# A decoder step on one core: key pages scored in pairs of visits, their projection's turned tiles moved one page and one score visit later

## The chip, the cores and the metric

One core of one Trainium2 chip runs the whole program. The metric is the device time of one execution in microseconds (us), lower is better. Of the kernel before three executions were timed: 908.4, 908.85 and 910.18 us, median 908.85 us.

## What is computed

One inference step of a two-layer decoder over 256 prompt tokens and 8 sequences of 8 sample tokens, all in float32. Layer one is an mLSTM mixer with an MLP, layer two block-sparse attention with an MLP. The change touches the attention of the sample tokens over 64 cached pages of 128 tokens (8 sequences of 8 pages), and the key projection that runs in its gaps:

```
kv = x @ w_kv                              # new keys and values, 320 tokens
q = (x @ w_q_b[j]).reshape(B, L, H_B, HD_B)
k_past = cache_k[page_table]               # 64 pages, 128 tokens x 8 heads x 128
page_sums = k_past.astype(F32).sum(2)      # block means choose 3 of 4 past blocks
lg_sel = einsum('bqhd,bqhrkd->bqhrk', q, sel_k) * scale - slope * dist
p = softmax(concatenate([lg_sel, lg_own])) # then times the value pages
```

## The kernel before

Activations lie transposed (features on partitions, T = 320 tokens along the free dimension). Each float32 product of a dense layer is three products of rounded parts: `dense` (L614 on) makes an output tile of 128 features from 8 chunks, each with a matmul high x high (L624), low x high (L625) and high x low (L626), 24 in all. ScalarE rounds a weight tile (`w_hi`, L1232), VectorE subtracts to get the rest (`w_lo`, L1636). Each of the five engines has its own hand-written queue, executed in order; semaphores tie the queues together.

The stretch of the change is the **key-page stage**. Pages come by DMA, issued by SyncE in a fixed order, into a ring of places. For page P TensorE does eight 128x128 transposes (`turn_page`, L1019), four heads into each of two PSUM banks; ScalarE copies the first bank into `k_turned` (`k_copy`, L1523), VectorE the second (L2031). Two pages are a *pair* (p = P // 2). `k_turned` has two buffers, one for even and one for odd pairs, so the copy of a page of pair p waits until pair p-2 is scored (`s_sc`). `score_pair` (L1061) multiplies the turned keys of one pair with the padded queries: matmuls whose weights are 32 columns wide, four heads side by side in the array, into banks 4 to 7. In the profile a score visit is 16 matmuls, in four groups of four.

In the gaps, for n = 0 to 7, `k_extra` makes head n of the new keys: at pair 2 + 2n TensorE runs the dense tile n of the key weights (*key tile*). VectorE then runs three operations on its bank (`kvq`, L1988 to L1990; only the first two read the bank), ScalarE adds the bias (`kvq` on its own queue, L1476), and one pair later (pair 3 + 2n) TensorE transposes the result in three pieces (`turn3`, L638 to L640: the *turned key tile*), which ScalarE copies out and stores with two DMAs that it issues itself (`kv_out`, L1461 to L1466). At pair 18 `own_scores` (L1030) stands in place of a key tile. Also on VectorE's queue here: logits of the first group of scores after pages 33 and 35 (L2058, L2060), a block maximum after page 39 (L2067, L2068), a dozen small operations after page 41 (L2074 to L2090), and after the even pages 10 to 24 a part of the residual is rebuilt (L1873 to L1877).

All transposes, key tiles, turned key tiles and own scores take their banks from one rotation over banks 0 to 3, the *slots*, in the order of the list `SLOTS`. Slot i may be written when what stood in slot i-4 has been read:

```
def slot_free(p, k):
    i = SLOT[p, k]
    if i >= 4:
        pe.wait_ge(*slot_read(*SLOTS[i - 4]))
```

`slot_read` says which semaphore tells of that reading: ScalarE's or VectorE's copy of a page half, for a key tile `s_uk` (raised after VectorE's third operation), for a turned key tile `s_tc`.

The order on TensorE before, for a pair p: both pages of p are turned, pair p-1 is scored, and then comes a key tile (even p from 2 to 16) or a turned key tile (odd p from 3 to 17).

After this stage come the value pages: `page_values` (L1119) uses each value page, the value projection runs in its gaps, then the rest of the layer.

Of the kernel before, what the change touches and what calls it, by code (L numbers as in the profile page):

```python
# [22 lines left out]
T = TP + TS  # L23
# [50 lines left out]


K_FIRST = 2
SLOTS = [(p, k) for p in range(NPG // 2) for k in range(5) if k < 4 or K_FIRST <= p <= K_FIRST + 16]
SLOT = {pk: i for i, pk in enumerate(SLOTS)}


# [82 lines left out]
def build(nc, x_prompt, x_sample, state_C, state_n, state_m, cache_k, cache_v, page_table,  # L163
# [4 lines left out]
    with ctx:  # L168
# [159 lines left out]
        def sem(name):  # L328
            return ctx.enter_context(nc.semaphore(name))
# [52 lines left out]
            sem(n) for n in ("k_copied_act", "k_copied_dve", "probs_turned_n", "probs_copied", "x_hi_prompt",  # L382
                             "o_scaled", "o_turned", "attn_out")]
        s_nm = sem("new_m")
        s_out = sem("stored")
        s_co, s_po = sem("c_stored"), sem("prompt_state_stored")

# [33 lines left out]
        def slot_read(p, k):  # L421

            if k < 4:
                return (s_kA, s_kD)[k % 2], 2 * p + k // 2 + 1
            n = (p - K_FIRST) // 2
            if n == 8:
                return s_ownr, 1
            return (s_uk, 8 + n + 1) if (p - K_FIRST) % 2 == 0 else (s_tc, n + 1)

        def emptied(t):  # L430

# [177 lines left out]
        def _(pe):  # L609
# [400 lines left out]
            def turn_page(P):  # L1010

                pe.wait_ge(s_in[PAGE_AT[P]], 16 * PAGE_LOADS[P])
                for half in range(2):
                    k = 2 * (P % 2) + half
                    slot_free(P // 2, k)
                    bank = slot_bank(P // 2, k)
                    for j in range(4):
                        h = 4 * half + j
                        last = nc.tensor.transpose(bank[:, 128 * j:128 * j + 128],  # L1019
                                                   page[PAGE_AT[P]][:, 128 * h:128 * h + 128], ident)  # L1020
                    last.then_inc((s_half, s_used)[half], 1)
# [13 lines left out]
            def k_extra(p):  # L1035

                n, odd = divmod(p - K_FIRST, 2)
                if p == K_FIRST + 16:
                    own_scores(p)
                elif odd:  # L1040
                    slot_free(p, 4)
                    pe.wait_ge(s_ev[0], evac(8 * Q_WK + n)[1])
                    turn3(slot_bank(p, 4), KA[:, n, :]).then_inc(s_tp, 1)
                else:
                    i = SLOT[p, 4]
                    dense(8 * Q_WK + n, XH, XL, None, TW, slot_read(*SLOTS[i - 4]))

            def score_pair(pair):

                G, bb, r = pair // 16, pair // 4 % 4, pair % 4  # L1050
                pe.wait_ge(s_kA, 2 * pair + 2)
                pe.wait_ge(s_kD, 2 * pair + 2)
                if pair % 16 == 0:
                    pe.wait_ge(s_qz, G + 1)
                if pair == 0:
                    pe.wait_ge(s_uk, 8)
                if pair in (16, 18):
                    pe.wait_ge(s_Lr, 2 + pair - 16)
                for a_ in range(2):
                    for j in range(4):  # L1060
                        last = mm(ps[SCORE_BANK[2 * a_ + r // 2]][32 * j:32 * j + 32,  # L1061
                                                                  256 * (r % 2):256 * (r % 2) + 256],
                                  QZ[G][:, 4 * a_ + j, bb, :], KT[pair % 2][:, 4 * a_ + j, :],
                                  start=(bb == 0 and r % 2 == 0), stop=True, skip_group_check=True)
                last.then_inc(s_sc, 1)
# [76 lines left out]

            for pair in range(NPG // 2):
                turn_page(2 * pair)
                turn_page(2 * pair + 1)
                if pair >= 1:
                    score_pair(pair - 1)
                if K_FIRST <= pair <= K_FIRST + 16:
                    k_extra(pair)
            score_pair(NPG // 2 - 1)  # L1150
            probs_turn(0)
            v_tile(0)
# [60 lines left out]
        def _(act):  # L1213
# [360 lines left out]
            for P in range(NPG):  # L1574
                p = P // 2
                k_copy(P)
                if P == 0:
                    kvq(7)
                if P in (1, 3):
                    q_lay(P // 2)  # L1580
                if P % 2 and K_FIRST <= p <= K_FIRST + 16:
                    k_extra(p)
                if 45 <= P < 55:
                    exp_step(0, P - 45)
# [42 lines left out]
        def _(dve):  # L1627
# [353 lines left out]
            def kvq(i):  # L1981

                t = 8 * Q_WQ + i
                u, bank = UK[i % 2], dense_bank(t)
                dve.wait_ge(s_mm, t + 1)
                if i >= 2:
                    dve.wait_ge(s_ev[0], evac(t - 2)[1])
                V.tensor_scalar(cb[:, t % 4:t % 4 + 1], bank[:, T + 1:TW], QSCALE if i < 8 else 1.0, None, ALU.mult)  # L1988
                own(V.scalar_tensor_tensor(u[:, :], nmu[:, :], bank[:, T:T + 1], bank[:, 0:T], ALU.mult, ALU.add))
                V.tensor_tensor(u[:, :], u[:, :], rs[:, :], ALU.mult).then_inc(s_uk, 1)  # L1990

            for i in range(8):
# [322 lines left out]
```

## Time and profile before

| | |
|---|---|
| timed executions | 908.4, 908.85, 910.18 us (median 908.85) |
| profiled execution, its own span | 909.7 us |
| key-page stage, first transpose to last score | 423.09 to 548.89 us of the span |
| TensorE matmuls busy | 896.8 us (99%) |
| TensorE weight loads busy | 838.1 us (92%) |
| VectorE / ScalarE busy | 622.7 us (68%) / 438.1 us (48%) |
| bytes moved | 182.78 MB, mean 201 GB/s |

The profile is of one execution. Times in its views count from the start of the span. In a row of the timeline, `x16` merges 16 instructions of one form, the first number is the start of the first, the second the time from there to the end of the last; what stands in brackets is idle time of the engine before it and what ended it. Matmuls overlap, so the distance between two starts tells what one costs, not its length. PE is TensorE, PEld its weight loads, DVE VectorE, ACT ScalarE, SP SyncE; a q behind a name is the engine's queue of instructions that issue or wait.

### The profile page before, as it was taken

The numbers are of one execution on the slowest core, as the hardware profiler recorded it, in microseconds if no ns is written. First come the engines' busy times: TensorE is split into PE (matmuls) and PEld (weight loads), VectorE is DVE, ScalarE is ACT, GpSimd is POOL, SyncE is SP. The second block draws the span as 40 slices with busy tenths as digits, with TensorE's granted clock in tenths as the row PEclk, the third lists the DMA queues.
The fourth block names the chain that finished last, engine by engine and source line by source line (L and its number), as shares of the span: only waits on it lengthen the run. The fifth ranks groups of instructions, "written<-read, shape, count | busy, mean of one in ns | idle before, by whom it ended". The sixth has DMA issues, their size and how long they took to land.

```text
span 909.7 us, 18709 instructions
## 1 busy us (share of the span) xinstructions
PE 896.8 (99%) x7472; PEld 838.1 (92%) x7472; DVE 622.7 (68%) x1089; ACT 438.1 (48%) x826; POOL 64.7 (7%) x81
## 2 busy tenths in 40 slices
PE   9999999999999999999999999999999999999996
PEld 8999988999999999999888878987999999999985
DVE  6477568788976575677575847446578897757536
ACT  5445666476345363445344453345447644526421
POOL 0010006500000000330000000000230000000000
PEclk9999999999999999999999999999999999999999
DMA  9982215664454444566988997998944545454401
GB/s 285 265 250 95 94 48 138 188 196 140 140 178 146 139 142 159 167 219 231 334 292 282 360 373 283 399 400 352 284 144 144 179 132 195 148 169 148 139 1 59
DMA packets 132331, 182.78 MB, mean 201 GB/s; under 512 B 5875, under 2 KB 113211, under 8 KB 132244
## 3 DMA queue, kind: packets, MB, share of 16 engines
q1 hardware_dynamic: 126938, 177.56, 59.0%
q0 software_dynamic: 640, 2.10, 0.9%
q10 hardware_dynamic: 4666, 1.92, 0.8%
q8 instruction: 60, 0.98, 0.4%
q14 instruction: 27, 0.22, 0.1%
HBM read 175.24 MB, written 6.32 MB: 200 GB/s over the span
## 4 chain that ended last, share of the span: by engine, by line
PE 94%; DMA 2%; SPq 1%; ACT 1%; DVE 1%; issue 1%; DVEq 0%
PE ps L624 24%; PE ps L626 23%; PE ps L625 23%; PE ps L1019 7%; PE ps L1061 4%; PE ps L1119 2%; DMA page<-in_cache_v_dram 2%; PE ps L907 1%; PE ps L909 1%; PE ps L908 1%; SPq L535 1%; SPq L542 1%; DMA x_tok<-in_x_prompt_dram 1%; PE ps L638 1%; PE ps L741 0%
## 5 line engine op out<-in xcount | busy, mean ns | idle before, releaser
L1232 ACT ACTIVATE w_hi<-raw 128x1024 fp32r<-128x1024 f32 x192 | 202.4, 1057 | 227.2 <-PE ps L626 204.4
L1636 DVE TENSOR_TENSOR w_lo<-raw,w_hi 128x1024 fp32r<-128x1024 f32 x192 | 237.4, 1240 | 102.7 <-ACT w_hi L1232 102.6
L624 PE MATMUL ps<-x_hi,w_hi 128*128 128x322 f32 (+1 forms) x888 | 279.8, 315 | 0.0
L626 PE MATMUL ps<-x_hi,w_lo 128*128 128x322 f32 (+1 forms) x888 | 276.5, 311 | 0.0
L625 PE MATMUL ps<-x_lo,w_hi 128*128 128x322 f32 (+1 forms) x888 | 276.1, 311 | 0.0
L624 PEld LDWEIGHTS ps<-x_hi,w_hi 128*128 128x128 f32 x888 | 168.1, 189 | 5.2 <-ACT k_turned L1523 2.9
L624 PE MATMUL ps<-h_hi,w_hi 128*128 128x320 f32 x552 | 170.9, 310 | 0.0
L626 PE MATMUL ps<-h_hi,w_lo 128*128 128x320 f32 x552 | 170.5, 309 | 0.0
L625 PE MATMUL ps<-h_lo,w_hi 128*128 128x320 f32 x552 | 170.4, 309 | 0.0
L625 PEld LDWEIGHTS ps<-x_lo,w_hi 128*128 128x128 f32 x888 | 168.8, 190 | 0.2
L626 PEld LDWEIGHTS ps<-x_hi,w_lo 128*128 128x128 f32 x888 | 167.6, 189 | 0.0
L624 PEld LDWEIGHTS ps<-h_hi,w_hi 128*128 128x128 f32 x552 | 103.8, 188 | 3.4 <-DVE x L1804 1.7
L625 PEld LDWEIGHTS ps<-h_lo,w_hi 128*128 128x128 f32 x552 | 103.8, 188 | 0.0
L626 PEld LDWEIGHTS ps<-h_hi,w_lo 128*128 128x128 f32 x552 | 103.7, 188 | 0.0
L1019 PE MATMUL ps<-base,page 128*128 128x128 f32 x512 | 63.1, 275 | 0.0
L1019 PEld LDWEIGHTS ps<-base,page 128*128 128x128 f32 x512 | 56.3, 141 | 7.1 <-issue 5.3
L2031 DVE COPY k_turned<-ps 128x512 f32<-128x512 f32 x64 | 43.8, 690 | 24.7 <-PE ps L1019 23.6
L1523 ACT ACTIVATE k_turned<-ps 128x512 f32<-128x512 f32 x64 | 36.1, 591 | 29.9 <-PE ps L1019 29.9
L1969 DVE TENSOR_TENSOR x<-x,ps 128x320 f32<-128x320 f32 x56 | 27.2, 487 | 31.8 <-PE ps L626 30.8
L1413 ACT ACTIVATE fm<-fm 128x320 f32<-128x320 f32 x64 | 29.4, 459 | 19.2 <-DVE fm L1936 19.1
L1934 DVE SCALAR_TENSOR_TENSOR fm<-ln_neg_mu,ps 128x320 f32<-128x320 f32 x64 | 35.0, 546 | 3.8 <-PE ps L626 3.7
L1936 DVE SCALAR_TENSOR_TENSOR fm<-ln_std,ps,fm 128x320 f32<-128x320 f32 x64 | 35.6, 556 | 2.3
(347 smaller groups left out, 978.7 us busy)
## 6 DMA issues: line engine op xcount, KB each, us to landing
raw<-in_w_up_dram SPq DMA_DIRECT2D x32, 1024.0 KB, 5.8
raw<-in_w_down_dram SPq DMA_DIRECT2D x32, 1024.0 KB, 5.2
page<-in_cache_k_dram SPq DMA_DIRECT2D x64, 512.0 KB, 5.7
page<-in_cache_v_dram SPq DMA_DIRECT2D x64, 512.0 KB, 9.4
raw<-in_w_in_a_dram SPq DMA_DIRECT2D x11, 1024.0 KB, 8.7
raw<-in_w_kv_dram SPq DMA_DIRECT2D x8, 1024.0 KB, 6.6
raw<-in_w_out_a_dram SPq DMA_DIRECT2D x4, 1024.0 KB, 5.2
raw<-in_w_q_b_dram SPq DMA_DIRECT2D x4, 1024.0 KB, 5.4
```

Source lines behind the costliest of these rows:

```text
L624: mm(out, WH[PLACE[t]][:, k, :], hi[:, k, 0:width], start=(k == 0), stop=False)
L625: mm(out, WH[PLACE[t]][:, k, :], lo[:, k, 0:width], start=False, stop=False)
L626: last = mm(out, WL[PLACE[t]][:, k, :], hi[:, k, 0:width], start=False, stop=(k == 7))
L1019: last = nc.tensor.transpose(bank[:, 128 * j:128 * j + 128], page[PAGE_AT[P]][:, 128 * h:128 * h + 128], ident)
L1061: last = mm(ps[SCORE_BANK[2 * a_ + r // 2]][32 * j:32 * j + 32, 256 * (r % 2):256 * (r % 2) + 256], QZ[G][:, 4 * a_ + j, bb, :], KT[pair % ...
L1232: A(WH[PLACE[t]][:, :, :], raw_tile(t), ACT.Copy)\
L1413: own(A(f[:, :], f[:, :], ACT.Relu))
L1523: A(KT[P // 2 % 2][:, 0:4, 128 * (P % 2):128 * (P % 2) + 128], slot_bank(P // 2, 2 * (P % 2))[:, :].rearrange("p (h t) -> p h t", h=4), AC ...
L1636: V.tensor_tensor(WL[PLACE[t]][:, :, :], raw_tile(t), WH[PLACE[t]][:, :, :].bitcast(F32), ALU.subtract)\
L1934: own(V.scalar_tensor_tensor(f[:, :], nmu[:, :], bank[:, T:T + 1], bank[:, 0:T], ALU.mult, ALU.add))
L1936: V.scalar_tensor_tensor(f[:, :], sd[:, :], bank[:, T + 1:TW], f[:, :], ALU.mult, ALU.add)\
L2031: V.tensor_copy(KT[P // 2 % 2][:, 4:8, 128 * (P % 2):128 * (P % 2) + 128], slot_bank(P // 2, 2 * (P % 2) + 1)[:, :].rearrange("p (h t) -> ...
```

## The change

TensorE visits the scores once in two pairs. At an even pair p (from 2 on) the order becomes: first page of p turned; pair p-2 and pair p-1 scored; the turned key tile that stood behind pair p-1; second page of p turned; the key tile. At an odd pair only its two pages are turned. The last visit scores pairs 30 and 31, as before. `SLOTS` and the queues of ScalarE and VectorE follow that order. A new semaphore `s_kb` is raised by VectorE's second operation on a key tile (the last that reads the bank) and takes the place of `s_uk` in `slot_read`.

```
 K_FIRST = 2
-SLOTS = [(p, k) for p in range(NPG // 2) for k in range(5) if k < 4 or K_FIRST <= p <= K_FIRST + 16]
+SLOTS = []
+for _p in range(NPG // 2):
+    SLOTS += [(_p, 0), (_p, 1)]
+    if K_FIRST < _p <= K_FIRST + 16 and _p % 2 == K_FIRST % 2:
+        SLOTS.append((_p - 1, 4))
+    SLOTS += [(_p, 2), (_p, 3)]
+    if K_FIRST <= _p <= K_FIRST + 16 and _p % 2 == K_FIRST % 2:
+        SLOTS.append((_p, 4))
...
-            return (s_uk, 8 + n + 1) if (p - K_FIRST) % 2 == 0 else (s_tc, n + 1)
+            return (s_kb, n + 1) if (p - K_FIRST) % 2 == 0 else (s_tc, n + 1)
...
             for pair in range(NPG // 2):
                 turn_page(2 * pair)
+                if pair % 2 == 0 and pair:
+                    score_pair(pair - 2)
+                    score_pair(pair - 1)
+                if pair % 2 == 0 and K_FIRST < pair <= K_FIRST + 16:
+                    k_extra(pair - 1)
                 turn_page(2 * pair + 1)
-                if pair >= 1:
-                    score_pair(pair - 1)
-                if K_FIRST <= pair <= K_FIRST + 16:
+                if pair % 2 == 0 and K_FIRST <= pair <= K_FIRST + 16:
                     k_extra(pair)
+            score_pair(NPG // 2 - 2)
             score_pair(NPG // 2 - 1)
...
-                if P % 2 and K_FIRST <= p <= K_FIRST + 16:
+                if P % 2 == 0 and p % 2 == 0 and K_FIRST < p <= K_FIRST + 16:
+                    k_extra(p - 1)
+                if P % 2 and p % 2 == 0 and K_FIRST <= p <= K_FIRST + 16:
                     k_extra(p)
...
-                own(V.scalar_tensor_tensor(u[:, :], nmu[:, :], bank[:, T:T + 1], bank[:, 0:T], ALU.mult, ALU.add))
+                ins = V.scalar_tensor_tensor(u[:, :], nmu[:, :], bank[:, T:T + 1], bank[:, 0:T], ALU.mult, ALU.add)
+                if 8 <= i < 16:
+                    ins.then_inc(s_kb, 1)
+                    dve.wait_ge(s_kb, i - 7)
+                else:
+                    own(ins)
```

**TensorE, behind a key tile.** Twelve rows before, from the first transpose after a key tile: `page2` and `page3` are the two pages of one pair, `k_turned`, `w_hi` and so on the tiles of the section above, ps0 to ps3 the four rotating banks.

```order
L1019 MATMUL ps3<-base_78,page2_134 128x128 [waits k_copied_dve,page_in2]
L1019 MATMUL ps3<-base_78,page2_134 128x128 x3
L1019 MATMUL ps0<-base_78,page2_134 128x128 [waits k_copied_act]
L1019 MATMUL ps0<-base_78,page2_134 128x128 x3
L1019 MATMUL ps1<-base_78,page3_135 128x128 [waits k_copied_dve,page_in3]
L1019 MATMUL ps1<-base_78,page3_135 128x128 x3
L1019 MATMUL ps2<-base_78,page3_135 128x128 [waits kvq_scaled]
L1019 MATMUL ps2<-base_78,page3_135 128x128 x3
L1061 MATMUL ps4<-k_turned0_128,q_padded0_170 32x256 [waits k_copied_dve,k_copied_act]
L1061 MATMUL ps4<-k_turned0_128,q_padded0_170 32x256 x3
L1061 MATMUL ps5<-k_turned0_128,q_padded0_170 32x256 x4
L638 MATMUL ps3<-base_78,k_attn_68 128x128 [waits act_emptied,k_copied_act]
```

The same place in the changed kernel (its lines are 8 higher):

```order
L1027 MATMUL ps3<-base_78,page2_134 128x128 [waits turn_copied,page_in2]
L1027 MATMUL ps3<-base_78,page2_134 128x128 x3
L1027 MATMUL ps0<-base_78,page2_134 128x128 [waits k_copied_act]
L1027 MATMUL ps0<-base_78,page2_134 128x128 x3
L1027 MATMUL ps1<-base_78,page3_135 128x128 [waits k_copied_dve,page_in3]
L1027 MATMUL ps1<-base_78,page3_135 128x128 x3
L1027 MATMUL ps2<-base_78,page3_135 128x128 [waits k_bank_read]
L1027 MATMUL ps2<-base_78,page3_135 128x128 x3
L1027 MATMUL ps3<-base_78,page4_136 128x128 [waits k_copied_act,page_in4]
L1027 MATMUL ps3<-base_78,page4_136 128x128 x3
L1027 MATMUL ps0<-base_78,page4_136 128x128 [waits k_copied_dve]
L1027 MATMUL ps0<-base_78,page4_136 128x128 x3
```

The score visit that stood behind `page3` is gone from there, and `page4` follows at once (two score visits stand behind it), into ps3, the bank that `page2`'s first half took eight transposes before.

**ScalarE, the same stretch** (of the first cycle, whose banks have other numbers). Before: bias of the key tile, the two copies of the next pair, the copy-out of the turned key tile and its DMAs, the next copy.

```order
L1476 ACTIVATE k_attn_68<-kvq0_179,b_times_w_81 128x320 [waits kvq_scaled]
L1523 ACTIVATE k_turned1_129<-ps1 128x4x128 [waits pair_scored,page_half_turned]
L1523 ACTIVATE k_turned1_129<-ps3 128x4x128 [waits pair_scored,page_half_turned]
L1461 ACTIVATE turned0_158<-ps1 128x256 [waits turn_done]
L1462 ACTIVATE turned0_158<-ps1 64x128
L1464 DMA out_5_dram<-turned0_158 128x2x128 [waits turn_copied]
L1466 DMA out_10_dram<-turned0_158 64x128
L1523 ACTIVATE k_turned0_128<-ps2 128x4x128 [waits pair_scored,page_half_turned]
```

In the changed kernel (lines 12 higher):

```order
L1488 ACTIVATE k_attn_68<-kvq0_179,b_times_w_81 128x320 [waits kvq_scaled]
L1535 ACTIVATE k_turned1_129<-ps1 128x4x128 [waits pair_scored,page_half_turned]
L1535 ACTIVATE k_turned1_129<-ps3 128x4x128 [waits pair_scored,page_half_turned]
L1535 ACTIVATE k_turned0_128<-ps1 128x4x128 [waits pair_scored,page_half_turned]
L1473 ACTIVATE turned0_158<-ps3 128x256 [waits turn_done]
L1474 ACTIVATE turned0_158<-ps3 64x128
L1476 DMA out_5_dram<-turned0_158 128x2x128 [waits turn_copied]
L1478 DMA out_10_dram<-turned0_158 64x128
```

The copy-out of the turned key tile stands one page copy later, and ps1 is read twice by page copies with one copy between them.

## Rows read from the trace of the kernel before

**Rows 1.** Windows (stretch, length, busy time of each engine, clock, DMA share, GB/s).

```profile
503.61:548.89 45.28, 45.28 (x534) 33.58 (x531) 28.47 (x52) 22.74 (x53) 0.00 (x0) 1.00 0.97 371
552.00:556.00 4.00, 4.00 (x58) 3.81 (x60) 3.97 (x8) 1.90 (x4) 0.00 (x0) 1.00 0.16 65
560.00:620.00 60.00, 58.82 (x1001) 52.58 (x1004) 30.14 (x89) 22.82 (x64) 2.31 (x8) 1.00 1.03 395
```

**Rows 2.** Timeline of TensorE over one cycle of two pairs, pages 10 to 13.

```profile
444.26 2.05 PE L1019 MATMUL ps<-base,page 128*128 128x128 f32 x16
446.25 1.07 PE L1061 MATMUL ps<-k_turned,q_padded 128*32 128x256 f32 x16
447.25 0.33 PE L638 MATMUL ps<-base,k_attn 128*128 128x128 f32 x1
447.41 0.27 PE L639 MATMUL ps<-base,k_attn 128*128 128x128 f32 x1
...
447.63 1.92 PE L1019 MATMUL ps<-base,page 128*128 128x128 f32 x16
449.48 1.07 PE L1061 MATMUL ps<-k_turned,q_padded 128*32 128x256 f32 x16
450.48 0.41 PE L624 MATMUL ps<-x_hi,w_hi 128*128 128x322 f32 x1
450.74 0.31 PE L625 MATMUL ps<-x_lo,w_hi 128*128 128x322 f32 x1
450.88 0.31 PE L626 MATMUL ps<-x_hi,w_lo 128*128 128x322 f32 x1
```

**Rows 3.** Timeline: second and last group of four of one score visit.

```profile
446.48 0.40 PE L1061 MATMUL ps<-k_turned,q_padded 128*32 128x256 f32 x4
446.92 0.40 PE L1061 MATMUL ps<-k_turned,q_padded 128*32 128x256 f32 x4
```

**Rows 4.** Waits, 423 to 549 us (who <- for whom: us in total, times, longest).

```profile
PEld ps L1019 <- DVE kvq L1990: 1.3, 8, 0.2
```

**Rows 5.** Timeline of VectorE and ScalarE behind the key tile that ends at 444.26.

```profile
444.46 0.16 DVE L1988 TENSOR_SCALAR b_times_w<-ps 128x1 f32<-128x1 f32 x1 [1.61 <-PE ps L626]
444.54 0.54 DVE L1989 SCALAR_TENSOR_TENSOR kvq<-ln_neg_mu,ps 128x320 f32<-128x320 f32 x1
445.11 0.49 DVE L1990 TENSOR_TENSOR kvq<-kvq,ln_rstd 128x320 f32<-128x320 f32 x1
...
445.64 0.56 ACT L1476 ACTIVATE k_attn<-kvq,b_times_w 128x320 f32<-128x320 f32 x1 [4.05 <-DVE kvq L1990]
446.11 1.06 ACT L1523 ACTIVATE k_turned<-ps 128x512 f32<-128x512 f32 x2
```

**Rows 6.** Timeline of ScalarE: copies after the turned key tile, next weight tile.

```profile
449.43 1.09 ACT L1523 ACTIVATE k_turned<-ps 128x512 f32<-128x512 f32 x2 [1.06 <-PE ps L1019]
450.40 1.06 ACT L1232 ACTIVATE w_hi<-raw 128x1024 fp32r<-128x1024 f32 x1
```

**Rows 7.** Timeline of VectorE around the last key tile: first logits, weight tile, key tile.

```profile
500.09 0.69 DVE L2058 TENSOR_REDUCE soft_small<-ps 128x2 f32<-128x512 f32 x1 [0.34 <-PE ps L1061]
...
502.61 1.22 DVE L1636 TENSOR_TENSOR w_lo<-raw,w_hi 128x1024 fp32r<-128x1024 f32 x1
503.81 0.16 DVE L1988 TENSOR_SCALAR b_times_w<-ps 128x1 f32<-128x1 f32 x1
```

**Rows 8.** Timeline of VectorE: copies of pages 40 to 43 and what stands between them.

```profile
512.89 2.28 DVE L2067 TENSOR_REDUCE soft_small<-logits 128x8 f32<-128x2048 f32 x1
...
515.39 1.29 DVE L2031 COPY k_turned<-ps 128x512 f32<-128x512 f32 x2
...
518.53 1.28 DVE L2031 COPY k_turned<-ps 128x512 f32<-128x512 f32 x2
```

**Rows 9.** Timeline of TensorE: the own scores.

```profile
509.71 0.63 PE L1030 MATMUL ps<-k_attn,q_attn 128*32 128x64 f32 x32
```

**Rows 10.** Waits of SyncE's queue, 552 to 640 us.

```profile
SPq L542 <- PE ps L1119: 5.7, 1, 5.7
```

More of the change, by code:

```diff
@@ L384, in build @@
         s_nm = sem("new_m")
+        s_kb = sem("k_bank_read")
         s_out = sem("stored")
```

## Prediction

> **What bounds the kernel now.** I read the windows first, then TensorE's timeline, then the queues that feed it. Over the last part of the key-page stage TensorE is busy in every microsecond, at the full 2.4 GHz (granted clock 1.00) [rows 1]: the stage lasts as long as TensorE's own queue, so I price the change there. Its timeline [rows 2] shows one cycle of two pairs: 16 transposes from 444.26, a score visit from 446.25, the turned key tile from 447.25, 16 transposes from 447.63, a visit from 449.48, and the next key tile from 450.48. The reader is to look at distances between starts. In the steady stream a transpose costs 0.11 us. Where a full-width stream changes to the 32-column scores and back, the distances grow, though the views call the engine busy: 16 transposes take 447.63 to 449.48, 1.85 us, where 16 x 0.109 would be 1.74.
>
> One real wait stands in this stretch: 1.3 us in eight waits of TensorE for VectorE's third operation on a key tile [rows 4]. It is the last quarter of the first block, 444.26 to 446.25 = 1.99 us against 1.85 for the other block.
>
> **What a merged visit saves.** Entering the scores costs 1.85 - 1.74 = 0.10. Inside a visit the groups are (446.92 - 446.48) / 2 = 0.22 apart, but from the last group to the next full-width matmul it is 447.25 - 446.92 = 0.33: 0.11 for leaving [rows 2, 3]. The first transpose after it takes 0.16 instead of 0.11 (447.25 to 447.41), 0.05; the first matmul of a key tile 0.26 instead of 0.15 (450.48, 450.74, 450.88), 0.11 [rows 2]. The visit's first group is longer by 0.02. So one change of width and back costs 0.29 before transposes, 0.33 before a key tile. Before there are 31 such excursions; after it 16 visits and one for the own scores, which then stand between transposes. 14 fewer; eight of them preceded a key tile: 14 x 0.29 + 8 x 0.04 = **-4.4 us**.
>
> What this draining is, the Trainium skill says ("TensorEngine Tiling (Array Packing)", Key Properties): changing the tiling mode drains the array. "TensorE: Matmul & The Clock Gate" (Single matmul latency) gives the part of a lone matmul that is not streaming as (398/2.4) = 166 ns; at that price for each of 28 changes of mode the gain would be an estimated 4.6 us, about what the rows give.
>
> **What the early signal saves.** VectorE's second operation ends at 444.54 + 0.54 = 445.08, the third at 445.11 + 0.49 = 445.60 [rows 5]. TensorE wants that bank after 12 transposes, at 444.26 + 1.30 = 445.56; it is free at 445.08 plus a signal of 0.05. The whole wait goes: the blocks' difference 1.99 - 1.85, up to 0.16 with rounding, eight times: **-1.2 us**. Behind the waiting instruction VectorE has nothing new, since it waited for its own second operation before too.
>
> **What the new order makes wait.** Here I follow the banks. Behind a key tile three pages are now turned in a row: the second and third slot of the rotation are fine, but the first bank of the third page (page 2p+4, for a key tile at pair p) is the one that the first half of page 2p+2 took eight transposes earlier, and it may be written only when ScalarE has copied that half. ScalarE's copy stands behind its bias of the key tile, and that one waits for VectorE's *third* operation, which the new semaphore does not make earlier. From the end of the key tile (444.26): third operation ends +1.34, bias starts +1.38, the two copies start at +1.85 [rows 5]. Two copies take 1.06 with 0.60 for one of them alone, so the first ends at about +2.44, and its signal reaches TensorE at +2.49. TensorE wants the bank after 16 transposes, at +1.74. It waits 0.75, and the first transpose after a wait pays the 0.05 of a restart: 0.80. Before, a score visit (1.00) and a different bank lay between, which is why this copy never showed as a wait. There are eight key tiles. Seven of these waits are alike: 7 x 0.80 = **+5.6 us**.
>
> **The eighth key tile** is worse. VectorE's queue has four logits operations and a weight tile between the copy of page 33 and this key tile: 500.09 to 502.61 and on to 503.81, 3.72 us, and before they ended just as the key tile did [rows 7]. They could start while page 33's score visit still ran. Now the key tile starts right after page 33's transposes. VectorE's copy of that page starts 0.20 later (the lag by which 444.46 follows 444.26) and frees the engine after 0.60 [rows 8]; then 3.72: it reaches the key tile's bank at +4.52 after the tile's start, where a tile of 24 matmuls, 0.15 apart, would have it at 3.60 + 0.20 = 3.80. Everything behind is 0.72 late. The second bank of page 35 is then wanted at +1.30 and free at 0.82 + 0.05 + 0.72 = 1.59, a wait of 0.29 and a restart; the first bank of page 36 is wanted at 1.74 + 0.34 = 2.08 and free at 2.49 + 0.72 = 3.21: 1.13 and a restart. Together **+1.5 us**.
>
> **Two single waits after it.** ScalarE issues the last turned tile's stores itself; in the present order it is free for a copy 449.43 - 447.25 = 2.18 after that tile starts [rows 2, 6]. Now page 37, the own scores and page 38 follow directly: the second bank of page 38 is wanted at 0.38 + 0.87 + 0.10 + 0.50 + 0.11 + 0.49 = 2.45 (the own scores take 0.63 to the end of the last, some 0.50 without its tail [rows 9]) and page 37's copy out of it ends at 2.18 + 0.60 + 0.05 = 2.83: about **+0.4**. And VectorE's block maximum and its dozen small operations after pages 39 and 41: from the start of the maximum to the next copy 518.53 - 512.89 = 5.64 [rows 8], with the copy of page 39 before it (0.20 + 0.60) and that of page 42 after (0.69 + 0.05) 7.18 less overlaps, about 7.0. TensorE had 7.3 of work there with three visits; now it has page 40, one double visit (2.0), pages 41 to 43 and a half, 5.9 up to the second bank of page 44, which page 42 must have left: about 1.1 to 1.35, I take **+1.3**.
>
> In the rest of the stage four pages in a row take 3.5 us, and VectorE's copies are 0.60 apart (1.29 for two, 0.69 for one) under the 0.87 of a page: no wait. ScalarE's exponentials fit with them.
>
> **The sum.** -4.4 - 1.2 + 5.6 + 1.5 + 0.4 + 1.3 = +3.2; walking all three queues through the whole stage by the same durations gives +3.5. I take +3.4.
>
> **Does it reach the end?** Behind the stage the DMA engines fall idle (share 0.16) and then run full (1.03) for 60 us [rows 1]: the value pages' loads set the end of that stage. They begin when the first value page has been used: SyncE's queue waits 5.7 us there [rows 10]. That use moves with the key-page stage, so the loads start as much later, and the delay reaches the end whole.
>
> The profiled execution took 909.7, 0.85 above the median of 908.85; +3.4 gives 913.1 by the profile, **912.3 us** by the median. A measurement of this kernel tells 0.2%, 1.8 us, from no change.
>
> **Rivals.**
> *The wait on ScalarE's copy does not come (faster).* If the copy of page 2p+2 ended by +1.7, the 7 x 0.80 and some 0.8 of the eighth tile's would go: 3.2 - 6.4, -3.2, 905.7 us. The sign turns below a wait of about 0.35 per cycle. For it: the start of the copies is read behind a queue order that I take as unchanged. Against: the rows of the order show bias, then copy, on ScalarE, and the bias waits for the same semaphore as before. 0.07.
> *The two sides cancel.* The seven waits come, but the late VectorE terms (1.5 - 0.8, 0.4, 1.3) don't, and the visits save a little more, 0.33 each: -4.6 - 1.2 + 6.4, +0.6, 909.4 us. For it: they rest on margins of some tenths. Also that the value stage takes the delay up: were its loads not started by the stage's end, nothing would be seen. Together 0.17.
> *The key tile's own turn comes late each cycle (slower still).* ScalarE now rounds the next weight tile after the stores of the turned tile and one more copy: from my walk at 8.05 after the key tile's end, 1.06 long, then VectorE's 1.22 to 10.36, and the next key tile's result is wanted at 10.2 + 0.2 [rows 5 to 7]. The margin is 0.03 us; where the stores take 0.3 more, each cycle is 0.3 longer: 6 x 0.3, +5.2, 914.1 us. For it: nothing pulls the queue back. Against: 450.40 follows 449.43 by 0.97 throughout, so the durations hardly vary. 0.14.
>
> **How the numbers follow.** The forecast (slower by about 3.4) has 0.62, the slower rival 0.14: slower 0.76. Cancelling has 0.17, faster 0.07. The range leaves out the fast rival and part of the cancelling one: 909.2 (half the forecast sum undone and a low draw) to 914.8 (the slow rival and a high draw of the runs).
>
> **What would show it.** Right: eight new waits of TensorE before a transpose, ended by ScalarE's page copy, 0.7 to 0.8 each; the eight waits for VectorE's third operation gone; excursions to the scores 16; cycles of 10.2 us instead of 9.9; one wait of over 1 us for VectorE near page 44; the value stage moved as a whole. Wrong: cycles of 9.4 us (no bank wait), or a key stage longer by 3 us and an end that is not.

## The result and the profile after

The changed kernel took 913.03 us (median of seven executions, 912.19 to 916.63) against 909.71 us (seven, 908.4 to 911.18) for the kernel before in the same series: ratio 1.0042, interval 1.0028 to 1.0056. It is slower by 3.3 us; 912.3 and +3.4 were forecast. The profiled execution is one of its two longest, 916.63 us, with a span of 914.8, so every term below is read from stretches and not from the whole. (A span is 1.8 or 1.9 shorter than its execution's time in every run here. The span of 909.7 that the prediction started from thus belongs to a time near 911.5, and its "0.85 above the median" compared a span with a time.)

The stage from the first page's transpose to the first use of a value page grew from 555.05 - 423.09 = 131.96 to 560.29 - 422.94 = 137.35 us: +5.4 in this execution. TensorE's timeline of the cycle that answers to [rows 2], pages 10 to 13:

```profile
444.04 0.31 PE L634 MATMUL ps<-x_hi,w_lo 128*128 128x322 f32 x1
444.19 1.91 PE L1027 MATMUL ps<-base,page 128*128 128x128 f32 x16
446.83 1.06 PE L1027 MATMUL ps<-base,page 128*128 128x128 f32 x8 [0.73 <-ACT k_turned L1535]
447.82 1.93 PE L1069 MATMUL ps<-k_turned,q_padded 128*32 128x256 f32 x32
449.69 0.33 PE L646 MATMUL ps<-base,k_attn 128*128 128x128 f32 x1
...
450.07 1.04 PE L1027 MATMUL ps<-base,page 128*128 128x128 f32 x8
450.86 0.39 PE L632 MATMUL ps<-x_hi,w_hi 128*128 128x322 f32 x1
...
454.50 0.27 PE L1027 MATMUL ps<-base,page 128*128 128x128 f32 x1
```

The double visit runs from 447.82 to 449.69, 1.87 us; two single ones took 2.00 and their entries besides. That is the gain. The loss is the bracket, idle time ahead of the row's first transpose: 16 transposes behind the key tile TensorE stands for ScalarE's copy. From key tile's end to key tile's end it is 454.50 - 444.19 = 10.31 us, 9.88 before (444.26 to 454.14). ScalarE's side:

```profile
445.64 0.56 ACT L1488 ACTIVATE k_attn<-kvq,b_times_w 128x320 f32<-128x320 f32 x1 [2.35 <-DVE kvq L2009]
446.11 1.07 ACT L1535 ACTIVATE k_turned<-ps 128x512 f32<-128x512 f32 x2
```

These are the rows of before [rows 5] almost to the hundredth: ScalarE has not moved, TensorE has come to want its copy earlier. The waits of the stage (423 to 560 us; us in total, times, longest):

```profile
PEld ps L1027 <- issue: 10.7, 15, 1.2
...
PE ps L1027 <- ACT k_turned L1535: 6.4, 9, 1.0
...
PEld ps L1069 <- issue: 3.0, 17, 0.3
...
PEld ps L1027 <- DVE kvq L2003: 1.5, 2, 0.8
...
PE ps L1027 <- DVE k_turned L2050: 1.1, 1, 1.1
PE ps L1027 <- DVE kvq L2003: 1.0, 2, 0.6
```

TensorE's timeline has 16 score visits in the stage; the third row counts their entries and one stop of 0.33 within the last visit. The wait for VectorE's third operation [rows 4] is gone; the second operation (L2003) ends two. Nine waits for ScalarE's copies have come. The single ones stand where the prediction put them, behind the eighth key tile (508.94 and 510.64), in page 38 and in page 44:

```profile
508.94 0.66 PE L1027 MATMUL ps<-base,page 128*128 128x128 f32 x4 [0.59 <-DVE kvq L2003]
510.64 1.06 PE L1027 MATMUL ps<-base,page 128*128 128x128 f32 x8 [1.04 <-ACT k_turned L1535]
...
516.31 2.40 PE L1027 MATMUL ps<-base,page 128*128 128x128 f32 x20 [0.23 <-ACT k_turned L1535]
...
524.93 0.66 PE L1027 MATMUL ps<-base,page 128*128 128x128 f32 x4 [1.14 <-DVE k_turned L2050]
```

One cycle is longer than its sisters, 464.75 - 454.50 = 10.25 being followed by 11.3. ScalarE's and VectorE's rows there:

```profile
461.50 1.68 ACTq L1478 DMA_DIRECT2D out_dram<-turned  x1
463.28 0.60 ACT L1535 ACTIVATE k_turned<-ps 128x512 f32<-128x512 f32 x1 [2.23 <-issue]
463.78 1.05 ACT L1244 ACTIVATE w_hi<-raw 128x1024 fp32r<-128x1024 f32 x1
```

```profile
464.86 1.23 DVE L1650 TENSOR_TENSOR w_lo<-raw,w_hi 128x1024 fp32r<-128x1024 f32 x1 [2.73 <-ACT w_hi L1244]
466.00 0.15 DVE L2002 TENSOR_SCALAR b_times_w<-ps 128x1 f32<-128x1 f32 x1
```

The issue of the second store held ScalarE for 1.68 us, where it mostly takes 0.50. The copy, the weight tile and its rest follow one after another, and VectorE reaches the finished key tile (464.75) at 466.00, 1.05 late. TensorE's 24 transposes there take 4.61 instead of 3.56. A second such issue, 1.83 at 503.62, makes the eighth key tile's share larger by 0.5 (4.75 here, 4.24 in e4 and e5 below). Together these two make 1.5 us of this execution's loss.

Behind the stage nothing is given back in this pair of profiles: the value pages take 642.65 - 560.29 = 82.36 us from first to last, 637.52 - 555.05 = 82.47 before, with the DMA engines full [rows 1] (mean share 1.03 in this window too), and SyncE's queue waits as long as in [rows 10]:

```profile
565.00:625.00 60.00, 58.81 (x999) 52.67 (x997) 30.38 (x89) 22.60 (x63) 2.32 (x8) 1.00 1.03 391
```

```profile
SPq L550 <- PE ps L1127: 5.7, 1, 5.7
```

In the profiles of the experiments below this distance lies between 81.0 and 82.6 us, with no relation to the length of the stage before it. So a part of the delay of up to about one microsecond could be given back without being seen here.

### The profile page after: what moved, and what is told of

Read it like the earlier page. It is cut to its first block, busy times and chain, and to the rows that moved or that the text cites. A ratio compares the mean times of both kernels' runs of the same rounds, so it can differ in the third digit from the quotient of the medians.

```text
span 914.8 us, 18709 instructions
## 1 busy us (share of the span) xinstructions
PE 894.4 (98%) x7472; PEld 839.7 (92%) x7472; DVE 622.1 (68%) x1089; ACT 438.8 (48%) x826; POOL 64.8 (7%) x81
## 4 chain that ended last, share of the span: by engine, by line
PE 90%; ACT 2%; DVE 2%; issue 2%; DMA 2%; SPq 1%; ACTq 1%; DVEq 0%; POOL 0%; POOLq 0%
PE ps L632 23%; PE ps L634 23%; PE ps L633 23%; PE ps L1027 4%; PE ps L1069 3%; PE ps L1127 2%; DMA page<-in_cache_v_dram 2%; ACT k_turned L1535 1%; PE ps L915 1%; PE ps L917 1%; PE ps L916 1%; ACTq L1478 1%; PE ps L646 1%; PE ps L663 1%; PE ps L749 0%
```

## The experiments

All eleven were timed; each median stands beside that of the kernel before in the same series. Line numbers in the fences are each kernel's own. "Stage" is the distance from the first page's transpose to the first value page's use in the profiled execution: 131.96 before, 137.35 with the change.

**The change in two halves.** First the early signal alone, in the old order.

```
# kernel before, with the new semaphore only
-            return (s_uk, 8 + n + 1) if ...
+            return (s_kb, n + 1) if ...
...
+                if 8 <= i < 16:
+                    ins.then_inc(s_kb, 1)
...
```

> The kernel before with the early signal alone (VectorE's second operation frees the key tile's bank), order unchanged. My theory: the eight waits of TensorE before the second bank of the page behind a key tile go, 0.10 to 0.16 us each: 0.9 to 1.2 us faster than before. Rival (the wait is only moved to the next slot, or the value stage's loads set the end anyway): no difference, the key-page stage as long as before.

Measured: 908.41 us against 909.9, ratio 0.999 (0.9977 to 1.0003); stage 131.39, 0.57 shorter, about half of what was expected. All eight waits are gone (16 transposes behind a key tile 1.84 instead of 1.99), but in four cycles the *other* block grew from 1.84 to 2.00. TensorE and VectorE in one of them:

```profile
445.11 2.06 PE L1020 MATMUL ps<-base,page 128*128 128x128 f32 x16
```

```profile
444.26 0.55 DVE L1875 SCALAR_TENSOR_TENSOR x<-x,ln_cols_alpha,ln_rstd 128x320 f32<-128x320 f32 x1
444.85 0.39 DVE L1878 TENSOR_SCALAR x<-x,ln_cols_alpha 128x320 f32<-128x320 f32 x1
445.27 0.69 DVE L2037 COPY k_turned<-ps 128x512 f32<-128x512 f32 x1
```

The rebuilt piece of the residual stands between two copies. TensorE's own wait had hidden it; with the wait gone the copy at 445.27 is the late one. Then the new order alone, with the old signal:

```
# changed kernel, without s_kb
-            return (s_kb, n + 1) if ...
+            return (s_uk, 8 + n + 1) if ...
...
-                if 8 <= i < 16: ...
+                own(V.scalar_tensor_tensor(u[:, :], ...))
```

> The changed kernel without the early signal: the new order alone. My theory: the second bank of page 2p+3 is late again by 0.15, but the wait for ScalarE's copy before page 2p+4 ends at the same moment as with the signal and swallows it: as slow as the changed kernel (3 to 3.5 us over before), waits for ScalarE's copy 0.6 instead of 0.75 each. Rival (the signal has its full worth in the new order): 1.2 us slower than the changed kernel, 4.5 over before.

Measured: 912.91 us, ratio 1.004 (1.0025 to 1.0054), no different from the whole change. The 24 transposes behind a key tile take the same 3.56 in six of the eight cycles (4.28 behind a store issue that was held 1.36, and 4.25 behind the eighth key tile). TensorE's idle time before ScalarE's copy is 0.51 instead of 0.66: the two delays end at the same copy. The late signal costs nothing here: whatever TensorE loses on it in the second page, it would have lost a little later waiting for ScalarE. In the new order the signal's 1.2 us are not a gain at all, and the order alone is what makes the kernel slower.

**The disputed wait removed.** ScalarE's bias of the key tile moves behind the copy of the first half of the page that follows next.

```
# changed kernel; ScalarE's queue
-                    kvq(8 + n)
...
             k_copy(P)
+            if P % 2 == 0 and p % 2 and K_FIRST < p <= K_FIRST + 15:
+                kvq(8 + (p - 1 - K_FIRST) // 2)
```

> The changed kernel with one move on ScalarE's queue: the copy of page 2p+2 stands ahead of the key tile's bias. My theory (the loss is ScalarE's copy standing behind a bias that waits for VectorE's third operation): the eight waits for ScalarE go, 5.6 to 6.4 us; four cycles in which VectorE rebuilds a residual chunk between two copies then make the second score visit wait 0.5 each, +2.1: in sum 4 to 4.5 faster than the changed kernel, about 1 us faster than before. Rival (the loss is the merged visit itself, or the DMA queues): no change against the changed kernel, 3 to 3.5 over before, the waits reappear under another name.

Measured: 908.97 us against 909.9, ratio 0.9993 (0.998 to 1.0006), about 4 us below the change. The wait for ScalarE's copy is gone in all eight cycles: 24 transposes take 2.71, not 3.56, in six of them. The fourth (3.50, behind a store issue held 1.55) and the eighth (3.27) still wait for VectorE's late turn at the key tile. And in four cycles a new wait stands within the double visit, here 445.63 - 444.12 = 1.51 for the first half in place of 0.89:

```profile
444.12 1.07 PE L1069 MATMUL ps<-k_turned,q_padded 128*32 128x256 f32 x16
445.63 1.07 PE L1069 MATMUL ps<-k_turned,q_padded 128*32 128x256 f32 x16 [0.44 <-DVE k_turned L2051]
```

```profile
443.27 0.48 DVE L1888 TENSOR_TENSOR x<-x,ln_neg_mu 128x320 f32<-128x320 f32 x1
...
444.80 1.29 DVE L2051 COPY k_turned<-ps 128x512 f32<-128x512 f32 x2
```

It is the rebuilt piece again (443.27 to 444.80), ahead of the copies that the second score visit needs.

**The gain by itself.** The kernel before, with merged visits only from pair 20 on, where there are no key tiles, and VectorE's small operations after page 43 instead of 41: six excursions fewer and none of the suspected waits.

```
# kernel before
-                if pair >= 1:
+                if 1 <= pair <= 18:
                     score_pair(pair - 1)
...
+                if pair >= 20 and pair % 2 == 0:
+                    score_pair(pair - 2)
+                    score_pair(pair - 1)
...
-                elif P == 41:
+                elif P == 43:
                     left_out(0)
```

> The kernel before with merged visits only from pair 20 on, where no key tile is left (six visits fewer), and the small operations after page 41 moved behind page 43, so that no wait for VectorE comes. My theory: 0.29 us per visit saved, 1.7 us faster than before, the stage after page 39 in blocks of 4 pages in 3.6 and two visits in 1.87. Rival (entering and leaving the narrow scores is no cost of its own, or the value stage takes the gain up): no difference.

Measured: 908.28 us against 909.9, ratio 0.9979 (0.9965 to 0.9994); stage 130.27, 1.69 shorter, 0.28 per excursion:

```profile
511.76 2.84 PE L1019 MATMUL ps<-base,page 128*128 128x128 f32 x24
514.52 1.93 PE L1061 MATMUL ps<-k_turned,q_padded 128*32 128x256 f32 x32
516.39 3.71 PE L1019 MATMUL ps<-base,page 128*128 128x128 f32 x32
520.03 1.94 PE L1061 MATMUL ps<-k_turned,q_padded 128*32 128x256 f32 x32
```

520.03 - 514.52 = 5.51 us for two pairs; two single rounds took 5.80 (from 512.17 to 517.97 before). The "Key Properties" of "TensorEngine Tiling (Array Packing)" in the Trainium skill name the drain at a change of mode but give it no price; the one estimated from "TensorE: Matmul & The Clock Gate" (Single matmul latency), 2 x 0.166 = 0.33 per visit, is a fifth too high here. The measured 0.28 decides.

**The long store issue.** Two ways to take it out of the key tile's path: the stores issued by GpSimd, or the next weight tile rounded ahead of the stores.

```
# e4, changed kernel: kv_out without its DMAs; GpSimd's queue
+            for i in range(8):
+                pool.wait_ge(s_tc, i + 1)
+                pool.dma_start(p_k[0, :, i, :]..., KO[i % 2][:, 0:2, :]).then_inc(s_to[i % 2], 16)
+                pool.dma_start(s_k_rows[:, i, :], KO[i % 2][0:64, 2, :]).then_inc(s_to[i % 2], 16)
```

> The changed kernel with the stores of the turned key tiles issued by GpSimd instead of ScalarE. In the profiled execution of the changed kernel two of these issues took 1.7 and 1.8 us instead of 0.5 and held up ScalarE's next copy and weight tile, and the key tile's turn on VectorE came 1 us late. My theory: these delays are what separates the executions at 916.6 from those at 912.2 to 913.2; without them every execution is near 912.5, no cycle of the key-page stage longer than 10.4, all else as in the changed kernel. Rival (the spread comes from elsewhere, as from the DMA of pages): executions over 915 stay.

```
# e5, changed kernel; ScalarE's queue, ahead of the turned key tile
+                    if p < K_FIRST + 16:
+                        split_to(8 * Q_WK + (p - K_FIRST) // 2 + 2)
                     k_extra(p - 1)
```

> The changed kernel with ScalarE rounding the next weight tile ahead of the turned key tile's copy and stores, instead of behind them. My theory: VectorE's part of the weight tile is then done over 1 us before the key tile ends, a late store issue cannot delay it any more: median unchanged to 0.5 us better than the changed kernel (912.5 to 913), spread small, the eight waits of 0.75 for ScalarE's copy all there. Rival (the weight tile is no part of it): executions over 915 stay.

Measured: 913.83 (ratio 1.0041, 1.0024 to 1.0057) and 913.24 us (1.0034, 1.0018 to 1.0049), against 910.18. In both the seven cycles are 10.25 to 10.28 us and the eighth key tile's 24 transposes take 4.24 instead of 4.75, in e5 although two of its stores were held 1.42 and 1.72. So the chain from store to weight tile to key tile is shown, and it accounts for 1.5 us of the profiled execution. What it costs in the usual execution is not settled. The medians have not moved, but e2's profiled execution, which took that run's median time, has such a cycle too. The expectation that no execution over 915 would remain was wrong in both: e4 has 915.31 and 915.96, e5 has 915.26. The held stores are not what separates the long executions from the short ones. With the stores gone from ScalarE, page 38's wait is gone too (24 transposes there 2.77, else 3.21): that term of 0.44 was ScalarE's stores, as the prediction had it.

**All queues at once, badly.** Copy first, weight tile early, and VectorE's rebuilt pieces, logits, block maximum and small operations all placed anew; e6 also has GpSimd's stores.

```
# e8, beside the edits of e3 and e5; VectorE's queue
-                if P == 33:
+                if P == 34:
                     dve.wait_ge(s_sc, 16)
                     logits(0, 0)
+                elif P == 35:
                     logits(0, 2)
-                elif P == 35:
-                    logits(0, 1)
+                elif P == 38:
                     logits(0, 3)
...
```

> The changed kernel with the queues behind TensorE put in the new order's terms: ScalarE copies page 2p+2 ahead of the bias and rounds the weight tile ahead of the turned tile's copy-out; VectorE rebuilds residual chunks only behind the second copy of an odd pair, takes the four logits one by one behind pages 34, 35, 37 and 38, the block maximum behind page 40 and the small operations behind page 43. My theory: the saving of the visits and the signal (5.6 us) comes through but for some 1.5 us of waits left around pages 36 to 44: 3.5 to 4 us faster than before, cycles of 9.4 us. Rival (the value stage is bound by its loads and takes a gain up, though it passed a loss on): the key-page stage 4 us shorter and the time less than 1 us better.

> As the run before it (all queues in the new order's terms), with the stores of the turned key tiles issued by GpSimd. My theory: page 38's wait for ScalarE (0.4) goes too: 4 to 4.5 us faster than before. Rival (GpSimd's issues are slower or disturb VectorE's copies): slower than the run before it.

Measured: 910.09 (ratio 1.0003, 0.9984 to 1.0021) and 911.23 us (1.0007, 0.9988 to 1.0025), against 910.18; 3.5 to 4.5 us of gain had been expected. The cycles came down to 9.40, but the logits had been moved too far. In e6:

```profile
506.71 1.93 PE L1069 MATMUL ps<-k_turned,q_padded 128*32 128x256 f32 x32 [2.44 <-DVE logits L2076]
```

Pair 16 is scored into banks that the logits have to empty first, and TensorE waits 2.44 us for the second of them. I had followed the four rotating banks and forgotten the score banks. e8 has the same wait of 2.44, and its visit then takes 3.49 instead of 1.87. There the granted clock had fallen just as the wait ended (TensorE in e8, columns as in [rows 1]):

```profile
502.00:503.00 1.00, 0.00 (x0) 0.00 (x0) 1.00 (x2) 0.00 (x0) 0.00 (x0) 1.00 0.85 299
504.00:505.00 1.00, 1.00 (x16) 0.59 (x12) 0.00 (x0) 0.00 (x0) 0.00 (x0) 0.50 1.05 430
```

The whole visit ran at the lower level of 1.2 GHz, its groups 0.43 apart instead of 0.22. In e6 the clock stayed at 1.00 behind the same wait, and the visit took 1.87.

**All queues at once, fitted.** The edits of e3 and e5, the rebuilt piece one page away from the copies that are waited for (behind the second page of odd pairs and the first page of even ones), the small operations after page 43, and the logits where they were.

```
# changed kernel + e3 + e5; VectorE's queue
-                if P % 2 == 0 and 5 <= p < 13:
+                if P % 2 == p % 2 and 5 <= p < 13:
                     rebuilt(1, p - 5)
...
-                elif P == 41:
+                elif P == 43:
                     left_out(0)
```

> The changed kernel with the copy of page 2p+2 ahead of the bias and the weight tile rounded ahead of the turned tile on ScalarE, residual chunks rebuilt only behind the second copy of odd pairs, and the small operations behind page 43 instead of 41 on VectorE; the logits stay where they are (behind pages 33 and 35), since the visit after page 36 needs two of them. My theory: of the saving of 5.6 us only 0.4 + 0.3 + 0.4 of waits around pages 35 to 38 are paid: 4.4 us faster than before by the key-page stage, cycles of 9.4 us. Rival (gains are taken up by the value stage's loads, which only pass losses on): first transpose to first value page 4 us shorter, but the value stage longer by as much and the time within 1 us of before.

Measured: 903.45 us (903.1 to 905.39) against 910.19, ratio 0.9921 (0.9897 to 0.9945): faster than both kernels. The stage takes 548.10 - 420.73 = 127.37 us, 4.6 less than before, and the value pages take 82.60, as before: they do not take the gain up. TensorE, one cycle:

```profile
441.15 2.78 PE L1027 MATMUL ps<-base,page 128*128 128x128 f32 x24
443.86 1.93 PE L1069 MATMUL ps<-k_turned,q_padded 128*32 128x256 f32 x32
445.73 0.33 PE L646 MATMUL ps<-base,k_attn 128*128 128x128 f32 x1
...
446.11 1.04 PE L1027 MATMUL ps<-base,page 128*128 128x128 f32 x8
446.90 0.39 PE L632 MATMUL ps<-x_hi,w_hi 128*128 128x322 f32 x1
```

ScalarE behind the same key tile, with the copy now ahead of the bias that waits for VectorE:

```profile
441.78 0.60 ACT L1535 ACTIVATE k_turned<-ps 128x512 f32<-128x512 f32 x1 [2.47 <-PE ps L1027]
442.52 0.57 ACT L1488 ACTIVATE k_attn<-kvq,b_times_w 128x320 f32<-128x320 f32 x1
443.00 0.57 ACT L1535 ACTIVATE k_turned<-ps 128x512 f32<-128x512 f32 x1
```

TensorE's rows of this cycle have no bracket; what is left in the stage are 0.56 at the eighth key tile and 0.44 in page 38.

Two variants of it. e10 takes the last weight tile's share of VectorE out of the eighth key tile's way, and moves SyncE's load of the weight unit that waits for it behind page 47's:

```
# e9; VectorE's queue
-                    split_to(8 * Q_WK + n + 2)
+                    split_to(8 * Q_WK + min(n + 2, 8))
...
+                if P == 36:
+                    split_to(8 * Q_WK + 9)
```

> As the run before it, with VectorE's part of the ninth weight tile moved from ahead of the last key tile to behind page 36's copy, and SyncE's load of the weight unit that waits for it moved behind page 47's. My theory: the last key tile's turn comes in time, the waits at pages 35 and 36 go: 0.6 us better than the run before it, 5 us faster than before. Rival (the pages' loads, disturbed by the moved unit, come late): a wait of TensorE for a page's DMA after page 44, no better than the run before it.

Measured: 905.3 us (902.87 to 907.9), ratio 0.994 (0.9916 to 0.9963). The eighth tile's 0.56 is gone (24 transposes 2.71, stage 126.81), but the time is not better than e9's; the two can't be told apart. And e11 is the kernel before with only the early signal and the rebuilt pieces placed as in e9, without merged visits:

> The order of before, with the early signal and the residual chunks rebuilt only behind the second copy of odd pairs. The signal alone shortened the key-page stage by 0.6 us instead of 1.2, and four blocks of 16 transposes grew by 0.15 each behind a turned key tile in the cycles in which a chunk is rebuilt. My theory: with the chunk out of the way these four go too, the stage is 1.2 us shorter than before, the time 1.2 us better. Rival (the wait belongs to ScalarE): the four waits stay.

Measured: 908.57 us, ratio 0.998 (0.9965 to 0.9995); stage 130.94, 1.02 shorter. All blocks of 16 transposes behind a key tile or a turned key tile are 1.84 to 1.85 long now, which confirms the reading of e1. The 0.16 that is missing to the expected 1.2 stands at the first turned key tile, whose store was held 1.04: the next key tile waits for the ScalarE copy behind it. Against it e9's merged visits, with the queues fitted to them, are worth another 130.94 - 127.37 = 3.6 us.

**Where the spread comes from.** Executions of one kernel differ by up to 8 us, more than the effect. Their mean granted clock sorts them roughly: of the kernel before, over the series of the experiments, four at 0.999 took 907.9 to 909.5 us, five at 0.992 took 912.7 to 914.6. The traces show where, long ahead of the stage. In the changed kernel's profiled execution, TensorE (columns as in [rows 1]):

```profile
42.00:44.00 2.00, 2.00 (x24) 1.79 (x23) 0.32 (x2) 1.71 (x3) 0.00 (x0) 1.00 1.09 351
44.00:46.00 2.00, 2.00 (x11) 1.93 (x11) 1.45 (x9) 0.62 (x1) 0.41 (x1) 0.63 0.60 194
46.00:48.00 2.00, 2.00 (x10) 2.00 (x9) 1.90 (x3) 0.00 (x0) 2.00 (x2) 0.52 0.48 152
```

The profiled execution of the kernel before has the same stretch at a mean of 0.83 between 40 and 50 us; e9's is at 1.00 there:

```profile
40.00:50.00 10.00, 10.00 (x77) 9.60 (x77) 4.14 (x14) 4.18 (x6) 4.03 (x11) 1.00 0.92 288
```

In e6 it is another place, 10 to 15 us, after TensorE had waited for a token tile (0.81 us, until 8.05):

```profile
10.00:15.00 5.00, 5.00 (x18) 3.57 (x17) 1.74 (x4) 2.17 (x5) 0.00 (x0) 0.50 1.03 310
```

Accordingly the stage's first transpose lies between 420.7 (e2, e9) and 424.7 us (e6). These stretches stand ahead of the code that the change touches. They go with e6's median being worse than e8's: eleven of its twelve executions ran at 0.995 or less, for a reason that is not shown. That e8's stage is the longer one (132.70 against 131.06) is the slow visit above, 3.49 - 1.87 = 1.62.

The clock also says how much of e9's gain is its own. The two profiled executions differ by 909.70 - 902.86 = 6.8 us: 2.4 of them lie ahead of the stage (423.09 against 420.73), where the clock had fallen in the one and not in the other, 4.6 in the stage, and from the last value page on both take 272.2. The timed executions agree roughly. At a clock of 0.999 e9's three took 903.27 to 903.5 and the four of the kernel before have a median of 908.2, a difference of 4.8; its single executions at 0.998, 0.997 and 0.995 lie 4.0, 6.5 and 6.6 below the medians of before at those clocks. So some 4.6 us are e9's own, and the remaining 2 of the 6.7 between the medians are most likely the clock's.

## Why the prediction was right

**Time and sign.** 912.3 was forecast, 913.03 measured, within 909.2 to 914.8; slower, by 3.3 us where +3.4 was forecast. The step from the profile to the median rested on a span taken for a time, but the sum was added to the median and did not suffer. That the hit is this close is in part luck. In e5's profile, where no held store costs anything, the waits come to 9.3 where 8.8 were forecast (5.6, 1.5, 0.4 and 1.3), and the last score is 3.8 later; in e2's, with one held store, the stage is 4.5 longer. The value pages, whose time differs from profile to profile for reasons that are not shown, took 0.7 to 0.8 less there than in the profile of before. And at equal mean clocks of 0.997 to 0.999 the changed kernel's few executions lie 3.6 to 4.8 above those of before. The sign and the mechanism do not depend on this; the agreement to 0.1 us does.

**The gain, -4.4 and -1.2.** Right as a sum, if what the waits don't explain is put down to it. In the profiled execution the stage's extra 5.38 us up to the last score (131.25 against 125.87) plus the savings must be the waits, and these are, against 2.71 for 24 transposes without one: seven times 3.56 to 4.61, together +7.12; the eighth 4.75, +2.04; page 38 +0.44 (3.21 against 2.77); page 44 +1.36 (5.00 against 3.64). Together 10.96, so 5.58 was saved; 5.6 was forecast. e7 gives one excursion as 0.28 (forecast 0.29). What the sum hid is e2's finding: the signal's part is a gain only where nothing stands behind it. In the old order it brings 0.57, or 1.02 with VectorE's queue put right; in the new order nothing more is lost without it.

**Seven waits of 0.80.** Right in place and cause, and nearly in size: six cost 0.85 to 0.93 in the profile (the seventh is the long cycle), all ended by ScalarE's page copy, and e3, which only moved that copy ahead of the bias, made them vanish. That the seven were the decisive term is shown: e3 has all the savings and stands 4 us below the change.

**The eighth key tile +1.5, page 38 +0.4, page 44 +1.3.** 1.53 in e4 and e5, whose key tile no long store delays (2.04 in the profile of the change); 0.44, and ended by what was named, the stores, as e4 shows; 1.36. e7 and e9, with the small operations two pages later, take 3.64 there: that cause is shown too.

**The end moves with the stage.** Right within what can be seen: 82.36 against 82.47 us of value pages in this pair, 81.0 to 82.6 in all profiles. A gain of 4.6 in the stage reached the end too (e9).

**The rivals.** That the wait does not come is refuted by e3; that the sides cancel, by the medians. The slower rival was a mechanism that exists: the key tile's margin of 0.03 us. It was expected in every cycle, from stores that take 0.3 more; in fact it strikes a cycle in which a store issue is held over a microsecond, and costs 0.72 (e2) to 1.05 there. The forecast of cycles of 10.2 held for the others.

**What the prediction did not say.** That the waits come from the order of ScalarE's queue and not from merging. It was written down in the walk (the bias stands ahead of the copy and waits for the third operation), but treated as given. A few lines in that queue and VectorE's turn +3.3 into -6.7 (some -4.6 to -4.8 without the clock's share). And the rebuilt pieces, which the prediction never named, are the next cover: they show as soon as either wait in front of them goes (e1, e3).

## What to carry to other kernels

Merging visits on the engine that bounds the kernel takes away exactly the pauses in which other engines emptied its buffers: walk each buffer from its last reader to its next writer, and look on the reader's queue for an instruction ahead of it that waits for something else. Let copies that free a buffer go before work that nobody waits for yet, and after each wait removed look for the next one behind the same cover. If executions differ by more than the effect, compare stretches of the trace, or executions of equal clock, before trusting a median.

## What the hardware showed that I had not expected

A DMA issue on ScalarE's queue, 0.50 us as a rule (same instruction, same size), was held 1.36 to 1.83 in one or two of eight stores in the change, e2, e3, e5 and e10, and delayed all that stood behind it. The longest in the other kernels were 0.87 (e1) and 1.04 (e11); what holds such an issue is open. SyncE issues a page's load beside held ones (461.53 to 461.87 us beside the one of 1.68) and beside quick ones alike, so that alone doesn't tell them apart. The same stores issued by GpSimd took 0.54 or 0.55 in all eight cases in e4.

TensorE's granted clock fell to its lower level of 1.2 GHz (0.50) for stretches of 3 to 7 us in some profiled executions and not in others, with the same code ahead (the last microseconds of the program aside, where it fell in all): near 10, near 45, and in e8 at 503 us of the span. Ahead of the ones near 45 TensorE ran some 25 small matmuls (all but one of 8 rows, 8 to 72 columns); in e8 it had waited 2.44 us. "TensorE: Matmul & The Clock Gate" in the Trainium skill (Part 1) says that the gate follows how busy the engine has been. The fall in e8 agrees; that e6's clock stayed at 1.00 behind the same wait shows that the wait alone does not decide it. And the rows near 45 show that a view which calls the engine busy (2.00 of 2.00) doesn't exclude a fall.
